# State space constants computed during the projection, and three reordered stretches of one decoder layer

## The reference

```python
z = xn @ p['w_in']                      # [q | k | v | u], 3*768 + 256 columns
q = rope_partial(rmsnorm(q, p['q_norm']), pos) * (HEAD_DIM ** -0.5)
k = rope_partial(rmsnorm(k, p['k_norm']), pos)
# three head groups: windows (128,1), (512,4), (2048,16); softmax over their log denominators
dt = jnp.exp(p['ssm_log_dt'])[:, None]  # state space constants
mag = jnp.exp(lam_re * dt)
a_re = mag * jnp.cos(lam_im * dt)
a_im = mag * jnp.sin(lam_im * dt)
c = (a - 1) / lam                       # complex: weights of the input
h = associative_scan(a, c * (B u)); y = Re(C h) + D * u
ssm_out = zs * sigmoid(zs @ p['w_glu'] + p['b_glu'])   # zs = gelu(y)
mixed = concat(rmsnorm(attn), rmsnorm(ssm_out)) @ p['w_out']
```

## Time and profile before

| | us |
|---|---|
| median of 3 runs | 1944.77 |
| profiled execution | 1944.68 |
| its span | 1942.8 |
| PE busy | 1792.9 (92%) |
| DVE busy | 960.4 (49%) |
| ACT busy | 665.6 (34%) |
| POOL busy | 249.0 (13%) |
| mean granted TensorE clock | 0.962 |

### The profile page before, as it was taken

The page is one execution under the profiler, slowest core; times in us unless marked ns, Lnnn a source line. Parts: engine busy times, 40 slices in busy tenths (PEclk is TensorE's granted clock), DMA queues, the critical chain, the costliest instruction groups (busy, mean ns, idle before and its releaser), DMA issues. The chain is left out here.

```text
span 1942.8 us, 31346 instructions
## 1 busy us (share of the span) xinstructions
PE 1792.9 (92%) x12419; PEld 1633.8 (84%) x12419; DVE 960.4 (49%) x1929; ACT 665.6 (34%) x1559; POOL 249.0 (13%) x566
## 2 busy tenths in 40 slices
PE   5889999998586998999999989999999999999998
PEld 5888998986354998898678979899899899889996
DVE  5523524646556534653353264545555454454545
ACT  5424324444155323543432054233223223223230
POOL 1511611608221000000000000000000000000000
PEclk9999999998786999999999989999999999999999
DMA  4210110005242532200642112111211112112102
GB/s 151 61 47 32 47 39 26 4 5 158 47 144 85 196 97 77 77 23 27 197 127 74 44 34 56 54 47 34 65 33 56 43 33 66 33 33 66 32 23 90
DMA packets 136239, 125.66 MB, mean 65 GB/s; under 512 B 15722, under 2 KB 128434, under 8 KB 136116
## 3 DMA queue, kind: packets, MB, share of 16 engines
q1 hardware_dynamic: 130500, 109.74, 18.4%
q0 software_dynamic: 5632, 14.44, 2.3%
HBM read 112.79 MB, written 10.70 MB: 64 GB/s over the span
## 5 line engine op out<-in xcount | busy, mean ns | idle before, releaser
L2649 PE MATMUL bank<-XH,WH 128*128 128x352 f32 x1056 | 344.4, 326 | 1.0 <-PEq L1612 1.0
L2649 PE MATMUL bank<-XH,WL 128*128 128x352 f32 x1056 | 342.0, 324 | 0.0
L2649 PE MATMUL bank<-XL,WH 128*128 128x352 f32 x1056 | 341.1, 323 | 0.0
L1969 PE MATMUL bank<-WH,XH 128*128 128x256 f32 x768 | 223.9, 292 | 12.4 <-DVE WL L1836 7.4
L1969 PE MATMUL bank<-WL,XH 128*128 128x256 f32 x768 | 219.5, 286 | 0.0
L629 PE MATMUL bank<-WH,XH 128*128 128x256 f32 (+3 forms) x648 | 212.2, 328 | 7.7 <-DVE WL L433 7.7
L1969 PE MATMUL bank<-WH,XL 128*128 128x256 f32 x768 | 218.5, 285 | 0.0
L2557 DVE TENSOR_TENSOR hres<-hres,bank 128x512 f32<-128x512 f32 (+2 forms) x198 | 135.7, 686 | 158.2 <-PE bank L2682 158.2
L629 PE MATMUL bank<-WL,XH 128*128 128x256 f32 (+3 forms) x648 | 203.7, 314 | 0.0
L629 PE MATMUL bank<-WH,XL 128*128 128x256 f32 (+3 forms) x648 | 203.3, 314 | 0.0
L2649 PEld LDWEIGHTS bank<-XH,WH 128*128 128x128 f32 x1056 | 199.5, 189 | 2.7 <-issue 1.1
(11 more groups left out here) (494 smaller groups left out, 3260.0 us busy)
## 6 DMA issues: line engine op xcount, KB each, us to landing
wstage<-w_up SPq DMA_DIRECT2D x44, 512.0 KB, 5.3
ring<-cache_mem_kv SPq DMA_DIRECT2D x64, 256.0 KB, 3.8
dstage<-w_down POOLq DMA_DIRECT2D x22, 512.0 KB, 3.8
wstage<-w_in SPq DMA_DIRECT2D x10, 1024.0 KB, 5.3
ringS<-cache_kv_dil SPq DMA_DIRECT2D x16, 512.0 KB, 6.4
wstage<-w_xkv SPq DMA_DIRECT2D x8, 1024.0 KB, 5.8
ringS<-cache_kv_dil SPq DMA_DIRECT2D x48, 128.0 KB, 2.8
xin<-x_prompt SPq DMA_DIRECT2D x8, 512.0 KB, 3.5
```

What stands on the lines that cost most here:

```text
L1969: ins = nc.tensor.matmul(MM[s % 3][:r, 0:WB], x[:, k, cols], w[:, b % 2, k], start=k == 0 and i == 0, stop=k == KT - 1 and i == 2)
L2649: ins = nc.tensor.matmul(bank[3 * g + j][:, 0:CH], w[:, slot, k, P * g:P * g + P], x[:, k, CH * j:CH * j + CH], start=k == 0 and i == 0, s ...
```

## The change

Four parts, in the order of the program.

1. **Constants beside the projection.** ACT's and DVE's work on the constants, and POOL's table up to the power 64, move into block 2 of the projection (steps (2,0) to (2,5)), into buffers of their own. The two `Sin` stand at step (2,2). The norm buffer `zr` is reused every 8 tiles.
2. **Probabilities first.** In every step DVE copies the transposed probabilities before it masks scores, instead of after.
3. **Middle.** POOL only doubles the table from 64 to 128 and then frees the buffers in which it stood, for which the scaling of `CA` and two loads wait (`e_tab`). The transposes of `WBR`/`WBI` and the cache keys stand in another order, the `TZ` DMAs are issued after the ring's load 17 and not 19, and the squares and their sums of all groups stand late. In the mixing, `work` takes 14 tiles of attention ahead of y, DVE takes 4 rests ahead of the scaling of y and 4 in between, and `WL` of `w_out` is made by POOL.
4. **Cross.** Value loads use 12 buffers (8 of the ring, 4 of the key copies once all keys are scored) and not 8, then 4; `WH`/`WL` of the next weights are made after the last probabilities.

The core of the diff (of the moved constants, only the ACT part; the rest has the same instructions as before):

```diff
+            def step_sizes():
+                act.wait_ge(S["ld_lam"], S["n_lam"])
+                nc.scalar.activation(dt_[:], dt_[:], ACT.Exp).then_inc(p_dt, 1)
+
+            def magnitude_and_angle():
+                act.wait_ge(p_exp, 1)
+                nc.scalar.activation(sm[:, 1], sm[:, 0], ACT.Exp).then_inc(p_exp, 1)
+                act.wait_ge(p_ang, 1)
+                nc.scalar.activation(sm[:, 16], sm[:, 5], ACT.Sin).then_inc(p_sin, 1)
+                nc.scalar.activation(sm[:, 17], sm[:, 4], ACT.Sin).then_inc(p_sin, 1)
+
             for s in range(LAST):
                 b, t = s // TILES, s % TILES
                 turn, kind, n = b // 3, b % 3, rows(t)
+                if (b, t) == (PAIR, 0):
+                    step_sizes()
+                if (b, t) == (PAIR, 2):
+                    magnitude_and_angle()
...
                 for a in due(s, 3):
                     take_output(a)
+                for a in due(s, 2):
+                    take_probabilities(a)
                 for a in due(s, 0):
                     mask_and_max(a)
-                for a in due(s, 2):
-                    take_probabilities(a)
...
-        work = [("a", a) for a in range(12)] + [("y", t) for t in range(TILES)] + [("s", g) for g in range(G)] + \
-               [("a", a) for a in range(12, A)]
+        work = [("a", a) for a in range(14)] + [("y", t) for t in range(TILES)] + [("a", a) for a in range(14, 20)] + \
+               [("s", g) for g in range(G)] + [("a", a) for a in range(20, A)]
+        EARLY = 4
...
-            load_ring(RING, 20)
+            load_ring(8, 18)
             sp.wait_ge(tz, 4)
             sp.wait_ge(tz_zero, 1)
...
+            last = [y[:, :, 63:64].to_broadcast([P, GH, 64]) for y in E_half]
+            nc.gpsimd.tensor_tensor(t[0], E_half[0], last[0], ALU.mult)
...
+            nc.gpsimd.tensor_tensor(EI[:, :, 64:128], t[2], t[3], ALU.add).then_inc(e_tab, 1)
             nc.gpsimd.memset(TZ[:], 0.0).then_inc(tz_zero, 1)
...
             nc.scalar.preload_act_table_set("natural_log_exp_and_others")
-            act.wait_ge(ld_lam, S["n_lam"])
-            nc.scalar.activation(dt_[:], dt_[:], ACT.Exp).then_inc(p_dt, 1)
             nc.scalar.activation(st[:, :, 0], lsum[:], ACT.Ln).then_inc(lnp, 1)
-            act.wait_ge(p_exp, 1)
-            nc.scalar.activation(sm[:, 1], sm[:, 0], ACT.Exp).then_inc(p_exp, 1)
-            act.wait_ge(p_ang, 1)
-            nc.scalar.activation(sm[:, 16], sm[:, 5], ACT.Sin).then_inc(p_sin, 1)
-            nc.scalar.activation(sm[:, 17], sm[:, 4], ACT.Sin).then_inc(p_sin, 1)
...
+            squares(1)
+            take_keys(24, KPAIRS)
+            squares(2)
             act.wait_ge(mx, 1)
...
             dve.wait_ge(t_c, 1)
+            dve.wait_ge(e_tab, 1)
             pw = [y[:].rearrange("p d g -> p g d").unsqueeze(3).to_broadcast([P, GH, 9, 16]) for y in (PR, PI)]
...
-            sum_squares(0)
...
-            sum_squares(1)
-            sum_squares(2)
+            for g in range(G):
+                sum_squares(g)
...
+            for k in range(EARLY):
+                take_rest(k)
             dve.wait_ge(so_r, 1)
...
+                if j % 2:
+                    take_rest(EARLY + j // 2)
...
-            dve.wait_ge(S["w_first_hi"], 1)
-            nc.vector.tensor_tensor(S["WL"][:, 0], S["wstage"][:], S["WH"][:, 0].bitcast(F32), ALU.subtract)\
-                .then_inc(S["w_first"], 1)
...
-    LATE = 8
-    slot = [n % RING if n < 2 * NL - LATE else 4 + n % 4 for n in range(2 * NL)]
+    WIDE = RING + SLOTS
+    slot = [n % RING if n < NL else (n - NL) % WIDE for n in range(2 * NL)]
...
-                if v:
+                if 0 < v < NU - 1:
                     take_output(v - 1)
                 take_probabilities(v)
-                if v == NU - 2:
-                    dve.wait_ge(S["x_hi"], 1)
-                    nc.vector.tensor_tensor(WL[:, 0], wstage[:], WH[:, 0].bitcast(F32), ALU.subtract)\
-                        .then_inc(S["x_lo"], 1)
+            take_output(NU - 2)
+            dve.wait_ge(S["x_hi"], 1)
+            nc.vector.tensor_tensor(WL[:, 0], wstage[:], WH[:, 0].bitcast(F32), ALU.subtract).then_inc(S["x_lo"], 1)
```

More of the change, by code:

```diff
@@ L113, in block_project @@
     MM, TR, SC, OB = bank[0:3], bank[3:5], bank[5:7], bank[7]
+    lamR, lamI, dt_, Bin = S["ssm_in"]
+    sm, PR, PI = S["ssm_c"]
+    GH, CH = 8, 8
+    HALF = 64
+    E_half = [S["gain_bc"][:, 512 * j:512 * j + 512].rearrange("p (g n) -> p g n", g=GH) for j in range(2)]
+    spare = att[:, 0:NT].rearrange("p a n -> p (a n)")
+    INV_2PI = 1.0 / (2 * math.pi)
+    MAGIC = 1.5 * 2.0 ** 23
+    PI_A, PI_B, PI_C = 6.28125, 0.0019350051879882812, 3.019916050e-7
+    assert abs(PI_A + PI_B + PI_C - 2 * math.pi) < 1e-11
     BLOCKS = 9
@@ L283, in scale @@
                 pool.wait_ge(z_rt, q + 1)
-                sums, r, tmp = (zr[:n, x, q] for x in range(3))
+                sums, r, tmp = (zr[:n, x, q % 8] for x in range(3))
                 link(nc.gpsimd.tensor_scalar(tmp, sums, -0.5 / E, -0.5 * EPS, ALU.mult, ALU.add))
@@ L679, in block_middle @@
     NC = SEQ // CH
[L680 to L683, removed]
+    E_half = [gain_bc[:, 512 * j:512 * j + 512].rearrange("p (g n) -> p g n", g=8) for j in range(2)]
     NTL = [1, 4, 2]
@@ L964, in _, with take_weights @@
             take_u(3)
-            squares(0)
-            take_keys(0, 4)
+            take_keys(0, 2)
+            def take_weights(q):
+                act.wait_ge(t_b, q + 1)
+                nc.scalar.activation((WBR, WBI)[q // 2][:, 4 * (q % 2):4 * (q % 2) + 4],
+                                     QB[q][:].rearrange("p (g n) -> p g n", g=4), ACT.Copy).then_inc(wb, 1)
+            for q in range(3):
+                take_weights(q)
+            take_keys(2, 4)
             act.wait_ge(us_p, 1)
@@ L1064, in _ @@
             nc.scalar.activation(S["WH"][:, 0], S["wstage"][:], ACT.Copy).then_inc(S["w_first_hi"], 1)
-            for k in range(22, len(work)):
+            for k in range(23, len(work)):
                 take_head(k)
@@ L1401, in _, with transpose_weights @@
             transpose_u(3)
-            keys(0, 4)
+            keys(0, 2)
+            def transpose_weights(q):
+                for g in range(4):
+                    ins = nc.tensor.transpose(QB[q][:, P * g:P * g + P], (WBR, WBI)[q // 2][:, 4 * (q % 2) + g], ident[:])
+                ins.then_inc(t_b, 1)
+            pe.wait_ge(u_t, 4)
+            pe.wait_ge(bb, 1)
+            for q in range(3):
+                transpose_weights(q)
+            keys(2, 4)
             pe.wait_ge(ld_us, 16 * DT)
@@ L2012, in block_cross @@
         ss = sb("ss6", [P, 4])
-        r_ld = [sem(f"r_ld{i}") for i in range(RING)]
+        r_ld = [sem(f"r_ld{i}") for i in range(WIDE)]
         zero, qz = sem("zero"), sem("qz")
```

297 lines of the change are left out of this document (162 added, 135 removed).

## The result

The changed kernel takes 1968.99 us (median of four runs, 1960.71 to 1972.66); the kernel before took 1946.03 beside it. The ratio is 1.0109, with a 95% interval of 1.0087 to 1.0130: slower by 23 us. The profiled execution is the fastest of the four, 1960.71 us with a span of 1958.8.

A forecast was written before the change was run, and what follows sets the result against it. PE was taken to set the projection's pace (busy 392.69 of 441.80 us) and to wait in the middle block. 1944.68 + 35.5 - 4.6 - 11.7 - 3.4 gave 1960.5, called 1960; 8 in 10 from 1934 to 1990.

The forecast's parts named there:

- Table loads, 35.5 forecast: Projection: two more ACT table loads in each of 36 q and k tiles cost 35.5 us, bounds 19 to 59.
- The loop's 3.88: Plain projection steps: the way through a tile, two steps long, sets 3.88 us a step, 0.83 over before.
- 4.0, 4.6 and 5.0: Projection steps carrying attention, about 14 in three stretches: us lost to late rotations per stretch, 13.6 in all.
- Hidden loads: Rival in the projection: loads fit ACT's idle time, the kernel gets faster, 1925 us with no loss; chance 0.14 (1941 and less).
- The reload that the Trainium skill's rule leads one to expect: Projection: a single reload after the Sin serves both logarithm and exponential, so 1925 us would come true; no separate chance.
- Draining: Rival: each of 72 table switches also drains ACT by 1.38 us, another 99 us, 2059 in all; chance 0.02.
- The clock as a rival of its own: Projection: gaps lower PE's clock, 16 us in half of 36 steps; 1972 to 1985 us in all; chance 0.19.
- Probabilities first, -4.6: Projection: copying probabilities before masking scores removes five PE waits, 3.9 us, and 0.7 of transposes; bounds 0 and -7.3.
- the 2.70 wait: Projection, at 323.63: PE's longest wait for the probabilities' copy, given no gain because loads make the exponential later.
- Middle, -11.7: Middle block: moved constants, earlier scan, TZ DMAs and exponentials, and new mixing order save 11.7 us; bounds -7 and -17.
- the groups' statistics hold the weights: Middle block: late squares make statistics leave 16 to 18 us later, so weights start 5.5 to 8 us earlier, not 12.
- Cross, -3.4: Cross block: twelve buffers and moved WL save 5.0 us, about 1.6 comes back near its end; bounds 0 and -5.

The follow-up runs named there:

- e1: The changed kernel with one more line: behind the two Sin in the projection ACT chooses its logarithm and exponential table again; 1917.57 us, ratio 0.9852.
- e6: e1 with one table load, of the set already there, ahead of the logarithm in each of 36 tiles; 1937.57 us, ratio 0.9948.
- e2: The kernel before with only one Sin of 8 columns added on ACT at step (2,2) of the projection; 1994.13 us, ratio 1.0249.
- e7: The changed kernel, table loads and all, with DVE's division of att ahead of the norm and rotation; 1961.17 us, ratio 1.0069.
- e11: e1 with the squares and their sums back near where the kernel before had them; 1911.88 us, ratio 0.9823.
- e12: The kernel before with only the new cross block: 12 value buffers, WH and WL behind the last probabilities; 1942.49 us, ratio 0.9980.

## Why the prediction was right, and which of its terms were not

The forecast was 1960 and slower, the measured time 1969, for the reason that was given. By its terms:

*Table loads, 35.5 forecast: right in kind, too small.* e1 and the changed kernel differ by 51 us in medians and by 46.6 in the projections of their profiled executions. Copy by copy, the 24 intervals between plain steps, both weight copies among them, account for 21.7 of it (and 1.2 lie ahead of the first load, by chance); the prediction had 19.1 + 2.8 = 21.9. The loop's 3.88 a step was 3.83, and e6 shows that it is the loop. The steps with attention were priced at 13.6 and cost 23.6 (steps 29 to 32: 6.8; 45 to 59: 8.7; 72 to 74: 8.1). That is the term that was mis-sized: "4.0, 4.6 and 5.0", one load of 1.29 in most steps. The windows of these stretches, first in the changed kernel, then in e1 (a window's length, then PE's busy time):

```profile
178.21:212.31 34.10, 27.44 (x198) 26.68 (x198) 14.83 (x45) 23.47 (x56) 9.61 (x29) 0.85 0.19 61
260.92:363.43 102.51, 95.44 (x583) 92.06 (x584) 39.09 (x94) 48.52 (x126) 15.29 (x48) 0.93 0.10 31
411.86:437.19 25.33, 18.66 (x124) 16.36 (x124) 13.95 (x32) 14.84 (x41) 5.37 (x19) 0.87 0.02 7
...
176.99:204.33 27.34, 24.70 (x198) 23.62 (x198) 14.85 (x45) 12.87 (x48) 10.38 (x29) 0.94 0.22 75
241.63:335.41 93.78, 90.92 (x582) 87.35 (x582) 38.01 (x93) 32.42 (x114) 14.44 (x43) 1.00 0.10 33
373.46:390.63 17.17, 15.13 (x123) 13.61 (x122) 13.26 (x31) 9.37 (x36) 3.79 (x13) 1.00 0.03 11
```

PE idles 12.9 us more in them (4.0, 4.2 and 4.6), and it is busy 10.8 us more with the same products. So the forecast fits the waiting alone, which may be luck to this digit. The waits themselves were fewer and longer than one load in most steps: DVE's program is in order, so a late rotation holds the division (as the prediction said) but also the copy of probabilities and the masking behind it, and PE waited 3.00 and 3.66 us for divisions, longer than two loads. What was left out of this term is that PE works slower behind such waits: 190.9 to 197.6 is at 0.50. What these steps would take at the full clock no run shows. The bounds given (5 to 36) held the term.

*Hidden loads: refuted* by e1 and e2. *The reload that the Trainium skill's rule leads one to expect* ("ScalarE: Activation LUTs", section Table sets: the hidden batching unit: one load for a logarithm and an exponential): that rule names a set that holds both, and the rows after a `Sin` show a load before each function; with the set chosen by hand in e1, none. *Draining: refuted*, e2 is 47.8 over and not some 130.

*The clock as a rival of its own:* it took part, and not in the way it was put. Plain steps with gaps of 0.4 to 0.8 us between PE's products kept the full clock for the most part (0.96 from 212.31 to 260.92, where e1 has 1.00). It wasn't half of the 36 steps. But over the whole projection PE was busy 405.04 us for the 2736 instructions that took 388.45 in e1, 16.6 more, and the attention steps have 10.8 of that: a cost of the size of this rival's 16, in other places.

*Probabilities first, -4.6: too small.* 8 to 9 on the chip. I gave the 2.70 wait nothing, as the later exponential would take its place. e2 shows the reverse: with loads and the old order the longest wait for that copy is 5.6, and the changed kernel's is 3.0. The copy's place is worth no less with late exponentials than without: e2's projection is 12.1 us longer than the changed kernel's.

*Middle, -11.7: about right,* against -12.4 from median to median of the executions above; the -18.3 of this profile is partly chance. Here each stretch came some 3 us before its due: the scan 10.8 earlier in the block (forecast 7.3), its end 14.3 (10.8), PE's transposes of the probabilities 13.6, GELU 14.9 (8 to 10). In the median of the eight GELU came 11 earlier. The claim that the groups' statistics hold the weights stands, but they are not alone. The last of their four DMAs, issued at 572.72, lands at 574.97, and DVE is done with its earlier work at 574.98:

```profile
574.58 0.40 DVE L1321 TENSOR_TENSOR ysb<-ysb,glS 32x256 f32<-32x256 f32 x1
574.99 0.26 DVE L1324 TENSOR_TENSOR w<-al 128x96 f32<-128x96 f32 x1
```

In all nine executions with late squares the weights' first operation (`w`) starts 0.02 to 0.06 us behind that landing, and in e7 DVE idles 0.14 us for it; before, the statistics lay there 25 us earlier. The late squares hold the scores' sums through DVE's order as well, and both ways end at the same time. e11 clears both at once: the sums come 4.9 earlier than in e1 and the weights 5.1. It doesn't show what either is worth alone.

*Cross, -3.4:* 4.9 in the block, 2.5 of it back behind it; e12 has 2.6 net. That the block behind it would pay wasn't forecast, and the wait of 1.57, which the moved `WL` was to take, stayed.

The sum came out at 1960.5 against a profiled 1960.71, which owes something to luck: in that execution the projection with the loads cost 11.1 more than forecast (46.6 over e1's, with the 1.2 of chance), and all else gave 10.9 more (30.6 for 19.7), 6.6 of it in the middle, most of that chance. With the usual middle it would have taken some 1965 us, an estimate from 1960.71 and the 169.0 above. What stays open is the rest of why the changed kernel's other three runs are 7 to 12 us slower than the profiled one. Their mean granted clock was lower (0.957, 0.952 and 0.951, for 0.959). e2's profiled run is its median, and its extra sits in the same attention steps (14.50 and 10.28 us for steps 57 and 74, where the changed kernel's profile has 9.85 and 7.38), but e2 also lacks the swap, and of the changed kernel only the one execution was traced.

## What to carry to other kernels

Look at the compiled program of each engine for what the source doesn't say: one function of another table, put where time seemed free, left 36 tiles with two table loads each, and choosing the table again right behind it is one line. Price such a cost by the way through a tile and not by the engine's idle share: ACT was 38% busy in the projection, and a single load of 1.28 us a tile still cost about 20 us. And where an engine's program is in order, ask for each wait what stands behind it; a delay costs most where short operations that others wait for are queued behind the late one. Look at the busy time of the engine that waits, too: in the steps with attention PE's slower work (10.8 us) grew nearly as much as its waits (12.9). And before a difference by place is read from one profile each, compare the executions that have the same code there: this middle block took 163.9 to 170.0 us.

## What the runs showed of the hardware

A table load took 1.283 us at each of the 82 places, also where the table asked for was already there (e6), and the engine went on 0.01 to 0.02 us later where the function had nothing else to wait for. From 178 us on in the projection of the changed kernel PE ran at half clock in eight stretches of 3.4 or 6.8 us, which began from 0.8 us ahead of the end of a wait to 1.6 behind it; these waits were 1.54 to 4.11 us long, and three of 1.51 to 1.77 us had no such stretch. e1 has one there, behind 1.75 us of idling, and none behind 1.97. One load a tile cost about 20 us in all and two cost 51: the first was far from free, though ACT had 1.99 us to spare in each plain step.
